# Attention scores of two items in one run of 64-row products (hybrid encoder layer, one core)

## The reference, cut to what matters

```
def diff_attention(q, k, v, lam, rel_bias):          # 4 heads, 2 maps each, 64 wide
    for each block of 128 queries:
        s = q_block @ k.T * scale + bias              # per map: (128, S), contraction over 64
        p = softmax(s)
        a = p[map 0] - lam * p[map 1]
        o = a @ v                                     # (128, 128) per head
...
x = x + concat(rmsnorm(o_att), o_conv) @ w_out
x = x + hier_moe(rmsnorm(x))                          # 16 experts, top 2 of one group
x = x + sigmoid(x @ w_ple_gate) * rmsnorm(p @ w_ple_proj)
```

## Time and profile before

| | before |
|---|---|
| median of 3 runs | 605.79 us (604.62 to 607.21) |
| profiled execution, first to last instruction | 603.0 us |
| TensorE busy | 595.1 us (99%) |
| weight loads busy | 490.5 us (81%) |
| VectorE busy | 419.7 us (70%) |
| ScalarE busy | 329.1 us (55%) |
| granted TensorE clock | full (1.000) |

### The profile page before, as it was taken

One profiled execution on the slowest core, in us unless ns is written; L12 is line 12 of the kernel. 1 busy time (PEld: TensorE's weight loads), 2 busy tenths in 40 slices (PEclk: granted clock), 3 DMA queues, 4 the chain that ended last, 5 costly groups with the idle time before them and its releaser, 6 DMA issues.

```text
span 603.0 us, 8730 instructions
## 1 busy us (share of the span) xinstructions
PE 595.1 (99%) x3160; PEld 490.5 (81%) x3160; DVE 419.7 (70%) x781; ACT 329.1 (55%) x595; POOL 69.2 (11%) x109
## 2 busy tenths in 40 slices
PE   9999999999999999999999999999999999999997
PEld 6888979888888777787887887778888888888886
DVE  5523983353552565646778789899999999788863
ACT  6851030222232675656556566789999998971211
POOL 0340000000000000100100113241221221210000
PEclk9999999999999999999999999999999999999999
DMA  8945827120211412212323676999999999785611
GB/s 337 382 57 182 312 113 274 34 73 34 74 66 71 183 57 85 71 70 106 99 78 118 252 277 238 375 363 412 410 411 411 411 411 398 279 326 210 226 40 66
DMA packets 39042, 126.52 MB, mean 210 GB/s; under 512 B 6448, under 2 KB 7472, under 8 KB 38968
## 3 DMA queue, kind: packets, MB, share of 16 engines
q1 hardware_dynamic: 33224, 112.97, 51.4%
q0 software_dynamic: 4896, 12.59, 5.4%
q10 hardware_dynamic: 880, 0.41, 0.2%
HBM read 113.33 MB, written 23.10 MB: 226 GB/s over the span
## 4 chain that ended last, share of the span: by engine, by line
PE 79%; DMA 9%; DVE 6%; POOL 2%; ACT 2%; issue 1%; SPq 1%; ACTq 0%; DVEq 0%; POOLq 0%
PE bank L507 20%; PE bank L509 19%; PE bank L508 19%; PE bank L1926 7%; DMA w_raw<-in_w_in 4%; PE bank L1943 3%; PE bank L1962 3%; DMA x_T<-in_xT 2%; DMA row_scale<-x_rstd 2%; POOL bias_sb L800 2%; PE bank L537 2%; PE bank L538 2%; PE bank L539 2%; PE bank L2236 1%; PE bank L2077 1%
## 5 line engine op out<-in xcount | busy, mean ns | idle before, releaser
L502 DVE TENSOR_TENSOR w_split<-w_raw,w_split 128x1024 fp32r<-128x1024 f32 x33 | 40.5, 1230 | 22.4 <-ACT w_split L497 22.2
L507 PE MATMUL bank<-w_split,moe_xT 128*128 128x512 f32 x120 | 48.5, 404 | 0.7 <-DVE w_split L1697 0.7
L509 PE MATMUL bank<-w_split,moe_xT 128*128 128x512 f32 x120 | 47.0, 392 | 0.0
L508 PE MATMUL bank<-w_split,moe_xT 128*128 128x512 f32 x120 | 46.9, 390 | 0.0
L497 ACT ACTIVATE w_split<-w_raw 128x1024 fp32r<-128x1024 f32 x33 | 34.4, 1051 | 20.0 <-DMA w_raw<-in_w_in 19.9
L1017 ACT ACTIVATE sq_tmp<-bank 128x512 f32<-128x512 f32 x12 | 7.2, 598 | 69.2 <-PE bank L509 69.2
L984 ACT ACTIVATE s<-s,mn 128x512 f32<-128x512 f32 (+1 forms) x48 | 30.9, 645 | 19.9 <-DVE mn L1433 19.9
L486 DVE TENSOR_TENSOR w_split<-w_raw_more,w_split 128x1024 fp32r<-128x1024 f32 x32 | 38.0, 1217 | 2.7 <-ACT w_split L480 2.7
L507 PE MATMUL bank<-w_split,x3T 128*128 128x512 f32 (+1 forms) x104 | 39.4, 379 | 0.0
L509 PE MATMUL bank<-w_split,x3T 128*128 128x512 f32 (+1 forms) x104 | 38.9, 374 | 0.0
L508 PE MATMUL bank<-w_split,x3T 128*128 128x512 f32 (+1 forms) x104 | 38.8, 373 | 0.0
(11 more groups left out here) (321 smaller groups left out, 1595.2 us busy)
## 6 DMA issues: line engine op xcount, KB each, us to landing
w_raw<-in_w_moe SPq DMA_DIRECT2D x32, 512.0 KB, 15.7
w_raw_room<-in_w_moe SPq DMA_DIRECT2D x30, 512.0 KB, 16.7
w_raw_more<-in_w_moe SPq DMA_DIRECT2D x30, 512.0 KB, 17.2
w_raw<-in_w_in SPq DMA_DIRECT2D x23, 512.0 KB, 10.0
pick<-moe_rows SPq DMA_DIRECT2D x12, 512.0 KB, 5.4
bias_rows<-bias_table SPq DMA_DIRECT2D x1, 4096.0 KB
w_raw<-in_w_out SPq DMA_DIRECT2D x8, 512.0 KB, 3.4
toep<-bias_rows SPq DMA_DIRECT2D x4, 896.0 KB, 7.2
```

Source lines behind the costliest of these rows:

```text
L502: nc.vector.tensor_tensor(W[:, u % WS, 1], raw(u)[0], f(W[:, u % WS, 0]), ALU.subtract).then_inc(lo_done, 1)
L507: nc.tensor.matmul(out, hi, whi, start=first, stop=False)
L508: nc.tensor.matmul(out, lo, whi, start=False, stop=False)
L509: return nc.tensor.matmul(out, hi, wlo, start=False, stop=last)
```

## The change

`scores` is called for two items at once. Ahead of the rounds, `scores(0)` and `scores(1)` both stand behind the second tile of the V projection; in the rounds, `scores(w)` and `scores(w + 1)` stand at the start of each even round, and odd rounds begin with their filler. The set of an odd item comes one round earlier; the calls of ACT and DVE, the banks, the waits in `scores` and all products are what they were.

```diff
-                    if b == V_B and i % 2:
-                        if i == 1:
-                            for m in range(TJ[Q_B] + 2, TJ[K_B] + TILES):
-                                t_ready(pe, m)
-                        scores(i // 2)
+                    if b == V_B and i == 1:
+                        for m in range(TJ[Q_B] + 2, TJ[K_B] + TILES):
+                            t_ready(pe, m)
+                        scores(0)
+                        scores(1)
...
-                if 2 <= w < NI:
+                if 2 <= w < NI and w % 2 == 0:
                     scores(w)
+                    scores(w + 1)
                 chunk(w, 0)
```

## The result

The changed kernel takes 608.49 us (606.29 to 612.93, 20 runs) against 606.31 us (604.62 to 608.24, 20 runs) before: a ratio of 1.0034, 95% interval 1.0021 to 1.0047. It is slower by 0.34%, some 2 us, where no measurable change was forecast. The profiled execution spans 605.7 us, the one before 603.0. The forecast adds the two up again and is not touched by this.

A forecast was written before the change was run, and what follows sets the result against it. TensorE, busy 595.1 of 603.0 us, was taken as the bound. The terms -3.9 + 0.6 + 1.2 + 1.2 + 0.2 + 0.9 gave +0.2 (+0.1 unrounded), so 605.9 us, range 603.4 to 608.3.

The forecast's parts named there:

- The price of a merge: Score sets on TensorE: the second set of a run costs 0.87 us with 512 keys; a merge saves 0.32.
- Rival (b): The second set costs as much as a lone one, merges save nothing: 609.8 us; chance 0.09, shared with an unseen stall.
- 0.11 us per merge: Saving per merge on TensorE, estimated from the skill's drain time as two drains; total 2.3 us later than the forecast.
- The first pair, 0.39 saved: Items 0 and 1, ahead of the rounds: 1.26 us given back between two wide products, 0.87 paid, 0.39 saved.
- Round 3, 0.6 lost: ACT's chain up to `pv(2)` takes 4.8 us against TensorE's 4.2, so 0.6 us is lost.
- Rounds 4/5 and 6/7, 1.2 lost each: Waits before `conv_part` and `att_part` stay; each pair pays 0.87 us with nothing given back, losing 1.2 against the saving.
- Rounds 8 to 15: ACT keeps up, 3.7 us against 4.2, except 0.1 late in each of rounds 11 and 15: 0.2 us lost.
- Rounds 16 to 24: DVE's chain from the router holds back the last `turn_a`: 0.9 us lost; rounds 17 to 20 keep their saving.
- The signs: In the stage, TensorE's waits grow from under 1 to about 5 us, and its busy time falls by about 4.
- The total: Whole kernel: a span of 603.1 us and 2.8 us around it give 605.9, against the median of 605.79.
- my range: Whole kernel time from 603.4 to 608.3 us, allowing for missing stalls below and a dearer second set above.
- a stall that I had not seen: Anywhere in the kernel, an unforeseen stall making it slower; chance 0.09, shared with the rival of a dear second set.

The follow-up runs named there:

- x1_wait_moved: The changed kernel with TensorE's wait for the V tiles' copies moved from ahead of round 1 to before `pv(0)`; 606.7 us, ratio 1.0009 to the kernel before.
- x4_8_to_21: The kernel before with only the seven pairs from 8/9 to 20/21 in one run; 604.82 us, ratio 0.9969.
- x3_only_4_and_6: The kernel before with only the pairs 4/5 and 6/7 in one run; 608.65 us, ratio 1.0044.
- y2_8_to_19: The kernel before with only the six pairs from 8/9 to 18/19 in one run; 605.9 us, ratio 0.9954.
- y1_best: The kernel before with pairs 5/6, 7/8, 10/11, 12/13, 14/15, 16/17 and 18/19 in one run; median 604.48 us, ratio 0.9932.
- y3_before_again: The kernel before, unchanged, run again for a second trace; median 606.86 us, ratio 0.9974 to the kernel before's runs beside it.

## Why the prediction was wrong

- **The price of a merge** (0.32 us, 0.39 for the first; second set 0.87): right. The run of two takes 1.92 us, and at `pv(0)` of x1_wait_moved the pair 0/1 is 0.38 ahead. The seven pairs of x4_8_to_21 save 0.30 each in the mean, from 0.21 to 0.41. Rival (b), a dear second set, is out, and so is the 0.11 us per merge that the prediction sets beside its own 0.32.
- **The first pair, 0.39 saved:** this is the step that failed. I weighed what the waits behind sets of odd rounds would cost, but of the set of item 1 I took only the products on either side of it, as if it stood in a gap without waits. Behind it stands TensorE's wait for the copies of the V tiles ahead of round 1. The copy of the fourth tile begins when its last product is done and takes 0.69 us; the earlier trace rows leave out what ACT does there. Instead of 0.39 saved, the pair costs 0.85, a term of 1.24 us. Against x1_wait_moved it reads thus: the filler starts 1.37 us behind the V tile's last product (202.99 to 204.36) and not 0.23 (202.70 to 202.93), and its second product another 0.08 later. The listed wait of 0.98 is less because it counts only from the end of the product before.
- **Round 3, 0.6 lost:** 0.5, of which 0.42 is listed as waiting. `pv(2)` starts 4.69 us behind `pv(1)`, forecast 4.8. The sum took ACT's split with the 1.06 that it lasts, but the exps start 0.94 behind its start (215.58 to 216.52).
- **Rounds 4/5 and 6/7, 1.2 lost each:** right. From `pv(3)` to `pv(4)` nothing changed with a set less, likewise from `pv(5)` to `pv(6)`, and x3_only_4_and_6 measured both alone, 1.72 against 2 x 0.87. `conv_part` now starts 0.26 behind DVE's low part (227.04 to 227.30) and not 0.06, which costs nothing, since `pv(4)` goes by ACT's copy. The wait in round 7 reads 1.56 instead of 1.8, since a listed wait counts only from the end of the product before.
- **Rounds 8 to 15:** 1.13 us ahead from `pv(6)` to `pv(14)` (2.86 to 1.73), forecast 1.08. The sum is right, its parts are not: by pairs it is 0.40, 0.27, 0.20 and 0.27, forecast 0.32, 0.22, 0.32 and 0.22. That the sum comes out so close is partly luck.
- **Rounds 16 to 24:** the last `turn_a` is 0.45 us earlier than at `pv(14)` (1.73 to 1.28), forecast 0.40; the uncovered wait is 0.76. That rounds 17 to 20 keep their saving held here (0.69 from `pv(16)` to `pv(20)`, forecast 0.64), but not for a kernel that gets there earlier: y2_8_to_19, 1.4 us ahead at `pv(16)`, and y1_best, 2.6 ahead, each lost 0.3.
- **The signs:** TensorE's waits were to grow to about 5 us and did (5.1), but 1.0 of that is the wait that was missing and the others came out smaller than forecast. Its busy time was to fall by about 4 us and fell by 2.8. An estimate from the rows gives most of the difference: at each of the five waits the last product counts as busy for its whole 0.39 us instead of the 0.23 to the next start, 0.8 in all.
- **The total:** the stage was forecast at +0.1 and is +1.28; with the missing wait taken away it is +0.06. The median of 608.49 lies 2.6 us above the forecast of 605.9 and 0.2 us above my range. Of the 2.6, the missing term is 1.2, 0.5 is that the kernel before came out at 606.31 in 20 runs and not at the 605.79 of three, and 0.9 (0.8 by the ratio) is the part outside the stage that has no cause assigned. So the step that failed would by itself have given 607.1, inside the range, and that the median fell outside took the other two as well, which says nothing for or against the mechanism of the forecast. The range had room for longer stalls of the chains I had seen, and none for a wait that I had not looked for. The chance of 0.09 for a stall that I had not seen was too small for the same reason: five of the six terms were waits uncovered by the same edit, and that a sixth might exist was the main risk.

## What to carry to other kernels

A batch of work that is moved away from a wait gives back nothing until something else covers that wait, and the list of waits of the kernel before shows such waits only where the cover was too short. So go to each place that the batch leaves, list every wait of the next instruction from the order of the program (here `acc_bank_free` at round 1, `dve_conv_lo` at 5, `dve_mix_lo` at 7) and compare the end of its releaser with the end of the batch. Merges of the same kind, seven instead of twelve and put where they cover waits, won 2.7 us of the stage where the twelve lost 1.3.

## What the runs showed of the hardware

- Two sets of 64-row products in one run go through without a seam: 16 instructions in 1.92 us to the next product, against 1.07 for 8. So the second set costs 0.85 to 0.87 (x3_only_4_and_6 shows 0.87 at `pv(4)`), and a merge that no wait spoils saves 0.2 to 0.4 us (the seven pairs of x4_8_to_21, and 0.38 for the pair 0/1 in x1_wait_moved).
- A product that waited with nothing left ahead of it on TensorE started 0.25 us behind the end of its releaser in round 1 (204.11 to 204.36), 0.26 behind in round 5 (227.04 to 227.30) and 0.06 behind in round 7 (240.19 to 240.25). The end of a releaser alone does not give the start; the cause of the difference was not tested.
- After TensorE had been idle for 4.9 us, its granted clock read 0.50 for 5.5 us of products (y3_before_again, from 44.7 to 50.2), and those products started 0.43 us apart in place of 0.23. The waits of up to 1.6 us in the stage left the clock at full.
- The stage, in which no listed wait of TensorE is for a transfer, repeats to 0.02 us from trace to trace of one kernel (141.38 and 141.36; 142.66 and 142.65), while the input projection ahead of it differed by 6.4 us between two traces of the same program. With two traces of each kernel, differences of a tenth of a per cent can be read in this stage and not in the total.
